# Folding the two key blocks of sliding-window attention into one row, and moving two weight low-parts to GpSimd

## The chip, the cores and the metric

One core of one Trainium2 chip runs the whole program. The metric is the device time in microseconds. The core's engines run side by side, each with its own instruction stream in a fixed order: TensorE (PE in the profile), VectorE (DVE), ScalarE (ACT), GpSimd (POOL), and SyncE (SP), which issues the weight loads. They hand work to each other through semaphores.

## The reference, cut to what matters

The program is a two-layer decoder trunk on 256 tokens of width 1024: a retention layer and a sliding-window attention layer, each between two SwiGLU blocks. The change touches only the window attention, which in the reference is:

```
qi = jnp.arange(WINDOW)[:, None]              # WINDOW = 128
kj = jnp.arange(2 * WINDOW)[None, :]
rel = qi + WINDOW - kj
...
sc = jnp.einsum('bqkgd,bjkd->bkgqj', qx, kx) * scale
valid = (rel >= 0) & (rel < WINDOW) & (blk * WINDOW + kj - WINDOW >= 0)
sc = jnp.where(valid[None, None, None], sc, NEG_INF)
p = jax.nn.softmax(jnp.concatenate([sc, sink_logits], axis=-1), axis=-1)[..., :-1]
return jnp.einsum('bkgqj,bjkd->bqkgd', p.astype(vx.dtype), vx)
...
return o @ w_o
```

There are 16 query heads and 2 key heads. Token block 0 sees only its own 128 keys. Query q of block 1 sees keys q+1 to 127 of block 0 and keys 0 to q of block 1: always 128 keys, and each position within a block exactly once.

## The kernel before, in words

Activations lie transposed, features on the 128 partitions and 256 tokens along the row. Every fp32 weight is split in two fp32r parts: ScalarE rounds a unit of 128x2048 from `stage` to `w_hi` (`split`, L339), VectorE subtracts to get `w_lo` (`split`, L658), and TensorE makes the three products that matter. Both tiles have four slots; SyncE loads the next unit of a slot when `lo_ready` says that its low part is made. All order is written out by hand, one list of calls for each engine; there is no scheduler.

The attention stage is the function `attention()` of each engine. It works in six softmaxes: `TWO_0A`, `TWO_0B`, `TWO_1A`, `TWO_1B` (token block 1, two blocks of keys, four heads each; the first digit is the key head) and `OWN_0`, `OWN_1` (token block 0, one block of keys, eight heads). For each:

- TensorE writes the mask into the score banks with a matmul of the identity (`masks`) and adds the scores (`head_scores`).
- VectorE reduces the maximum (`softmax_front`, L1036) and makes the exponent's bias with three tiny operations (L1038 to L1040). ScalarE makes the exponentials and their sums (`exps`, L532). VectorE (or, for `TWO_0A` and `TWO_0B`, ScalarE, L543) divides by the sum (`softmax_back`, L1055).
- TensorE transposes the probabilities (`transposed_p`, L1585), ScalarE moves them to `pt_own` or `pt_two` (`rows_of_p`, L556), TensorE multiplies by the values (`values`), and ScalarE and VectorE split the result in two parts of `o_t` (L563; `out_lo`, L1062).
- `q_scale` on VectorE (a reduce, L907, and some ten tiny operations, L910 and L663 to L672) makes the scale of each query head; `q_rope` (L847 to L853) rotates the queries.
- `wo_tiles` on TensorE is the output projection, four weight units `wo` 0 to 3, each waiting for its `w_lo` and its `o_t` part.

GpSimd only adds up squares for the norms (L1166 to L1189); it does nothing between 760.1 and 823.2 us. In all texts "two-input" means a VectorE operation whose two tensor operands both lie in SBUF, such as L658, L853, L1038 or L1055, in contrast to a reduce or to an operation that reads PSUM.

## Time and profile before

| | |
|---|---|
| median of 3 runs | 1015.26 us (1015.19 to 1015.81) |
| the profiled execution | 1015.4 us, its span 1013.6 us |
| TensorE busy | 1009.5 us, 100% of the span; granted clock 1.00 throughout |
| VectorE, ScalarE, GpSimd busy | 786.3, 497.2, 101.4 us |
| attention stage on TensorE | 756.9 to 826.7 us |

The profiled execution's own time is longer than its span by what lies before the first and after the last instruction, 1.8 us. Times of single instructions below are in microseconds from the span's start.

### The profile page before, as it was taken

The numbers are of one execution on the slowest core, as the hardware profiler recorded it, in microseconds if no ns is written. First come the engines' busy times: TensorE is split into PE (matmuls) and PEld (weight loads), VectorE is DVE, ScalarE is ACT, GpSimd is POOL, SyncE is SP. The second block draws the span as 40 slices with busy tenths as digits, with TensorE's granted clock in tenths as the row PEclk, the third lists the DMA queues.
The fourth block names the chain that finished last, engine by engine and source line by source line (L and its number), as shares of the span: only waits on it lengthen the run. The fifth ranks groups of instructions, "written<-read, shape, count | busy, mean of one in ns | idle before, by whom it ended". The sixth has DMA issues, their size and how long they took to land.

```text
span 1013.6 us, 15818 instructions
## 1 busy us (share of the span) xinstructions
PE 1009.5 (100%) x5916; PEld 886.5 (87%) x5916; DVE 786.3 (78%) x886; ACT 497.2 (49%) x537; POOL 101.4 (10%) x103
## 2 busy tenths in 40 slices
PE   9999999999999999999999999999999999999998
PEld 8888888888888888888888888888897898888888
DVE  7988866797797878777767787787778977977743
ACT  7455435544443354454444454464447944544432
POOL 0000013201101052000013100001220041000000
PEclk9999999999999999999999999999999999999999
DMA  9664456652542454555455645535562344644461
GB/s 348 242 237 177 143 174 218 246 197 104 218 195 97 193 171 173 212 190 180 150 179 199 246 166 201 191 135 172 187 244 115 110 160 188 208 168 166 156 193 64
DMA packets 32295, 185.31 MB, mean 183 GB/s; under 512 B 3840, under 2 KB 6400, under 8 KB 16128
## 3 DMA queue, kind: packets, MB, share of 16 engines
q1 hardware_dynamic: 31968, 184.64, 50.9%
q8 instruction: 23, 0.38, 0.2%
q10 hardware_dynamic: 288, 0.16, 0.1%
q14 instruction: 16, 0.13, 0.0%
HBM read 183.73 MB, written 1.05 MB: 182 GB/s over the span
## 4 chain that ended last, share of the span: by engine, by line
PE 100%; DVE 0%; issue 0%; DVEq 0%
PE ps L1219 99%; PE ps L1585 1%; PE ps L1552 0%; PE ps L1544 0%; DVE x L841 0%; DVE ones L1125 0%; DVEq L1126 0%
## 5 line engine op out<-in xcount | busy, mean ns | idle before, releaser
L1219 PE MATMUL ps<-h,w_hi 128*128 128x512 f32 x1664 | 556.1, 393 | 0.0
L1219 PE MATMUL ps<-h,w_lo 128*128 128x256 f32 x1664 | 430.8, 279 | 0.0
L658 DVE TENSOR_TENSOR w_lo<-stage,w_hi 128x2048 fp32r<-128x2048 f32 (+1 forms) x190 | 398.2, 2105 | 29.3 <-ACT w_hi L339 29.1
L1219 PEld LDWEIGHTS ps<-h,w_hi 128*128 128x128 f32 x1664 | 310.1, 188 | 66.9 <-DVE w_lo L658 0.2
L339 ACT ACTIVATE w_hi<-stage 128x2048 fp32r<-128x2048 f32 (+1 forms) x190 | 326.7, 1727 | 5.6 <-PE ps L1219 4.7
L1219 PEld LDWEIGHTS ps<-h,w_lo 128*128 128x128 f32 x1664 | 302.1, 189 | 3.5
L1219 PE MATMUL ps<-act_t,w_hi 128*128 128x512 f32 (+1 forms) x726 | 240.0, 386 | 0.0
L1219 PE MATMUL ps<-act_t,w_lo 128*128 128x256 f32 x704 | 190.1, 279 | 0.0
L1219 PEld LDWEIGHTS ps<-act_t,w_hi 128*128 128x128 f32 x726 | 134.4, 188 | 28.4
L371 ACT ACTIVATE tmp<-ps 128x1024 f32<-128x1024 f32 x44 | 45.1, 1026 | 189.2 <-PE ps L1219 189.2
L1219 PEld LDWEIGHTS ps<-act_t,w_lo 128*128 128x128 f32 x704 | 130.4, 189 | 0.3
L740 DVE TENSOR_TENSOR tmp<-ps,tmp 128x1024 f32<-128x1024 f32 x44 | 53.8, 1223 | 68.4 <-ACT tmp L371 68.4
L404 ACT ACTIVATE tmp<-ps 128x256 f32<-128x256 f32 x39 | 14.8, 380 | 118.9 <-PE ps L1219 118.9
L1219 PE MATMUL ps<-w_hi,h 128*128 128x512 f32 x192 | 60.3, 395 | 0.0
L786 DVE SCALAR_TENSOR_TENSOR tmp<-ps,tmp 128x256 f32<-128x256 f32 x39 | 16.4, 421 | 53.9 <-ACT tmp L404 53.9
L376 ACT ACTIVATE tmp<-tmp 128x512 f32<-128x512 f32 x44 | 27.9, 633 | 61.9 <-DVE tmp L746 61.9
L746 DVE TENSOR_TENSOR tmp<-tmp,r_row 128x1024 f32<-128x1024 f32 x44 | 53.9, 1225 | 1.5
L1166 POOL TENSOR_TENSOR sq_sum<-x 128x256 f32<-128x256 f32 x5 | 3.1, 614 | 479.2 <-DVE x L788 416.2
L1175 POOL TENSOR_TENSOR sq_sum<-sq_sum,sq 128x256 f32<-128x256 f32 x31 | 45.3, 1461 | 2.4
L1219 PE MATMUL ps<-y_t,w_hi 128*128 128x512 f32 x128 | 43.3, 392 | 0.0
L1219 PEld LDWEIGHTS ps<-w_hi,h 128*128 128x128 f32 x192 | 35.1, 188 | 7.8 <-issue 0.7
L715 DVE SCALAR_TENSOR_TENSOR h<-x,gain,h 128x256 fp32r<-128x256 f32 (+1 forms) x48 | 32.5, 677 | 10.2 <-ACT h L350 10.2
(172 smaller groups left out, 746.9 us busy)
## 6 DMA issues: line engine op xcount, KB each, us to landing
stage<-w_in_dram SPq DMA_DIRECT2D x85, 1024.0 KB, 4.8
stage<-w_out_dram SPq DMA_DIRECT2D x64, 704.0 KB, 4.0
stage<-w_ret_dram SPq DMA_DIRECT2D x24, 1024.0 KB, 4.9
stage<-w_ret_out_dram SPq DMA_DIRECT2D x8, 1024.0 KB, 4.8
stage<-w_q_dram SPq DMA_DIRECT2D x4, 1024.0 KB, 6.3
stage<-w_o_dram SPq DMA_DIRECT2D x4, 1024.0 KB, 4.9
stage<-w_in_dram SPq DMA_DIRECT2D x8, 256.0 KB, 4.2
stage<-w_in_dram SPq DMA_DIRECT2D x2, 512.0 KB, 6.1
```

Of the source, the lines that this page charges most:

```text
L339: nc.scalar.activation(w_hi[:, s, 0:n], stage[:, s, 0:n], ACT.Copy).then_inc(hi_ready, 1)
L371: nc.scalar.activation(t, ps[:, 4 * (g % 2):4 * (g % 2) + 4, T:2 * T], ACT.Copy).then_inc(in_lo_half, 1)
L376: nc.scalar.activation(tmp[:, g % 2, 0:512], tmp[:, g % 2, 0:512], ACT.Silu).then_inc(in_silu, 1)
L404: nc.scalar.activation(tmp[:, d % 2, 0:T], ps[:, bank, T:2 * T], ACT.Copy, scale=scale).then_inc(out_lo_half, 1)
L658: nc.vector.tensor_tensor(w_lo[:, s, 0:n], stage[:, s, 0:n], w_hi[:, s, 0:n].bitcast(F32), ALU.subtract).then_inc(lo_ready, 1)
L715: nc.vector.scalar_tensor_tensor(h[:, ds(d + per * i, 1), T:2 * T], x[:, ds(d + per * i, 1), :], gain[:, ds(m * DT + d + per * i, 1)], h[: ...
L740: nc.vector.tensor_tensor(t, ps[:, 4 * (g % 2):4 * (g % 2) + 4, 0:T], t, ALU.add).then_inc(in_free, 1)
L746: nc.vector.tensor_tensor(t, t, same(r_row[:], 4), ALU.mult).then_inc(in_scaled, 1)
L786: chain.step(nc.vector.scalar_tensor_tensor(t, ps[:, bank, 0:T], scale, t, ALU.mult, ALU.add))
L1175: nc.gpsimd.tensor_tensor(sq_sum[:], sq_sum[:], sq[:], ALU.add).then_inc(sum_added, 1)
L1219: return nc.tensor.matmul(out_, w, x_, start=start, stop=stop)
L1585: last = nc.tensor.transpose(ps[:, P_T_BANKS[e][r], q * P:(q + 1) * P], s[:, h0 + head, kb * P:(kb + 1) * P], ident[:])
```

## The change

Three things change in the attention stage.

1. The rows with two key blocks are folded to 128 keys. The scores of both blocks are made without a mask. In PSUM, VectorE copies the first block's scores over those of the second wherever the second's key lies after the query (`copy_predicated`), and the maximum, exponentials, scaling and transposes work on 128 keys instead of 256. After the transpose, the folded probabilities lie in the second half of `pt_two`; GpSimd multiplies them by a 0/1 mask into the first half and subtracts that from the second (`blocks_of_p`). `values` waits for `p_second` instead of `pt_ready`.
2. The low parts of `wo` units 0 and 1 are made by GpSimd in four quarters each (`low_part`) instead of by VectorE; VectorE keeps a wait at a later place (`low_part_made`), which passes the news on to `lo_ready`.
3. ScalarE makes the high part of `wo` unit 1 before the last transposed queries instead of after the first probabilities.

```
-    s_two = [at(f"s_two{c}", [P, CH, 2 * P], F32, ...) for c in range(2)]
+    s_two = [at(f"s_two{c}", [P, CH, P], F32, ...) for c in range(2)]
...
@@ VectorE, softmax_front
-                chain.step(nc.vector.tensor_reduce(mx.rearrange("q (i p) -> q i p", p=2), scores_by_head(e), AX.X,
-                                                   ALU.max))
+                by_head = scores_by_head(e)
+                if b:
+                    chain.step(nc.vector.copy_predicated(
+                        by_head[:, :, :, P:2 * P],
+                        mask[:, P:2 * P].bitcast(I32).rearrange("q (i p k) -> q i p k", i=1, p=1).broadcast_to(
+                            [P, n // 2, 2, P]), by_head[:, :, :, 0:P]))
+                    by_head = by_head[:, :, :, P:2 * P]
+                chain.step(nc.vector.tensor_reduce(mx.rearrange("q (i p) -> q i p", p=2), by_head, AX.X, ALU.max))
@@ VectorE, attention
                 q_rope(1, 0)
-                split(u)
                 q_rope(1, 1)
                 softmax_back(OWN_0)
+                low_part_made(0)
                 q_scale(1, 0, 2)
                 softmax_front(OWN_1)
                 out_lo(0)
                 softmax_front(TWO_1A)
-                split(u + 1)
                 softmax_back(OWN_1)
+                low_part_made(1)
                 softmax_front(TWO_1B)
@@ GpSimd
+            def low_part(j):
+                u = FIRST["wo", 0] + j
+                pool.wait_ge(hi_ready, u + 1)
+                for q in range(4):
+                    cols = slice(q * UNIT // 4, (q + 1) * UNIT // 4)
+                    nc.gpsimd.tensor_tensor(w_lo[:, u % SLOTS, cols], stage[:, u % SLOTS, cols],
+                                            w_hi[:, u % SLOTS, cols].bitcast(F32), ALU.subtract).then_inc(wo_lo, 1)
+            def blocks_of_p(n, e):
+                c, b, h0, heads = SOFTMAXES[e]
+                first, second = (pt_two[:, h0:h0 + heads, kb, :] for kb in range(2))
+                pool.wait_ge(pt_ready[e][0], 1)
+                nc.gpsimd.tensor_tensor(first, second, same(mask[:, 0:P], heads), ALU.mult).then_inc(p_first, 1)
+                pool.wait_ge(p_first, n + 1)
+                nc.gpsimd.tensor_tensor(second, second, first, ALU.subtract).then_inc(p_second, 1)
@@ TensorE, attention (the four masks() of TWO_0A, TWO_0B, TWO_1A, TWO_1B go; so do the second transposes)
-                masks(TWO_0A)
...
                 transposed_p(TWO_1A, 0)
-                transposed_p(TWO_1A, 1)
@@ TensorE, values
-                    pe.wait_ge(pt_ready[e][0], 1)
-                    pe.wait_ge(pt_ready[e][1], 1)
+                    pe.wait_ge(p_second, 2 * c + k % 2 + 1)
```

How the streams change at the places that matter. First VectorE around the queries of the second key head; `w_lo` is the low part of `wo` unit 0, `s_own` the probabilities of `OWN_0`. Before:

```order
L847 TENSOR_TENSOR q_a<-ps,tables 128x512 [waits q_squared10,q_done1,qt_done00]
L850 TENSOR_TENSOR q_b<-ps,tables 128x8x32 x2
L853 TENSOR_TENSOR q_a<-q_a,q_b 128x512 [waits dve_chain]
L658 TENSOR_TENSOR w_lo<-stage,w_hi 128x2048 [waits hi_ready]
L847 TENSOR_TENSOR q_a<-ps,tables 128x512 [waits used,qt_done01]
```

The same place of the changed kernel:

```order
L846 TENSOR_TENSOR q_a<-ps,tables 128x512 [waits q_squared10,q_done1,qt_done00]
L849 TENSOR_TENSOR q_b<-ps,tables 128x8x32 x2
L852 TENSOR_TENSOR q_a<-q_a,q_b 128x512 [waits dve_chain]
L846 TENSOR_TENSOR q_a<-ps,tables 128x512 [waits used,qt_done01]
```

The subtraction of 2048 columns is gone from VectorE here. GpSimd, which had nothing between two norm sums, now has sixteen operations of 512 columns in this stage (changed kernel):

```order
L1209 TENSOR_TENSOR w_lo<-stage,w_hi 128x512 [waits hi_ready]
L1209 TENSOR_TENSOR w_lo<-stage,w_hi 128x512 x3
L1217 TENSOR_TENSOR pt_two<-pt_two,mask 128x4x128 [waits pt_ready00]
L1219 TENSOR_TENSOR pt_two<-pt_two 128x4x128 [waits p_first]
L1217 TENSOR_TENSOR pt_two<-pt_two,mask 128x4x128 [waits pt_ready10]
L1219 TENSOR_TENSOR pt_two<-pt_two 128x4x128 [waits p_first]
L1209 TENSOR_TENSOR w_lo<-stage,w_hi 128x512 [waits hi_ready]
L1209 TENSOR_TENSOR w_lo<-stage,w_hi 128x512 x3
L1217 TENSOR_TENSOR pt_two<-pt_two,mask 128x4x128 [waits pt_ready40]
L1219 TENSOR_TENSOR pt_two<-pt_two 128x4x128 [waits p_first]
L1217 TENSOR_TENSOR pt_two<-pt_two,mask 128x4x128 [waits pt_ready50]
L1219 TENSOR_TENSOR pt_two<-pt_two 128x4x128 [waits p_first]
```

On TensorE, the values of `TWO_1A` (the own block's 4 matmuls, then the two blocks' 8) before:

```order
L1219 MATMUL ps<-pt_own,v_sb 64x128 [waits pt_ready30]
L1219 MATMUL ps<-pt_own,v_sb 64x128 x3
L1219 MATMUL ps<-pt_two,v_sb 64x128 [waits pt_ready41,pt_ready40]
L1219 MATMUL ps<-pt_two,v_sb 64x128 x7
```

and in the changed kernel:

```order
L1254 MATMUL ps<-pt_own,v_sb 64x128 [waits pt_ready30]
L1254 MATMUL ps<-pt_own,v_sb 64x128 x3
L1254 MATMUL ps<-pt_two,v_sb 64x128 [waits p_second]
L1254 MATMUL ps<-pt_two,v_sb 64x128 x7
```

The place in TensorE's order is the same; the wait has moved from ScalarE's copy to GpSimd's second operation behind it.

## Rows read from the trace of the kernel before

**Rows 1.** Windows, columns: stretch, length, busy PE, PEld, DVE, ACT, POOL, clock, DMA, GB/s.

```profile
765.00:805.00 40.00, 39.89 (x291) 32.63 (x291) 36.80 (x91) 33.93 (x94) 0.00 (x0) 1.00 0.28 103
```

**Rows 2.** Timeline of TensorE: start, length, instruction, count.

```profile
764.21 0.62 PE L1219 MATMUL ps<-mask_r,ident_r 128*128 128x512 f32 x2
764.66 0.50 PE L1219 MATMUL ps<-ones,sq_sum 128*128 128x2 f32 x4
...
776.83 0.60 PE L1552 MATMUL ps<-ident,q_a 128*128 128x128 f32 x4
...
786.31 1.91 PE L1585 MATMUL ps<-ident,s_two 128*128 128x128 f32 x16
787.98 0.71 PE L1219 MATMUL ps<-mask_r,ident_r 128*128 128x512 f32 x2
...
794.20 0.74 PE L1219 MATMUL ps<-mask_r,ident_r 128*128 128x512 f32 x2
794.86 1.13 PE L1219 MATMUL ps<-k_t,q_t 64*128 64x256 f32 x8
796.11 0.47 PE L1219 MATMUL ps<-o_t,w_hi 128*128 128x256 f32 x2
...
806.62 1.04 PE L1585 MATMUL ps<-ident,s_two 128*128 128x128 f32 x8
...
810.21 1.04 PE L1219 MATMUL ps<-pt_two,v_sb 128*64 128x128 f32 x16
```

**Rows 3.** Timeline of VectorE in the attention stage; in brackets, idle before and releaser.

```profile
765.93 0.69 DVE L907 TENSOR_REDUCE hs<-q_sq 128x8 f32<-128x512 f32 x1 [0.57 <-ACT q_sq L517]
...
768.82 1.22 DVE L1036 TENSOR_REDUCE sm<-ps 128x4 f32<-128x1024 f32 x1
...
774.58 0.68 DVE L847 TENSOR_TENSOR q_a<-ps,tables 128x512 f32<-128x512 f32 x1
...
775.96 0.69 DVE L853 TENSOR_TENSOR q_a<-q_a,q_b 128x512 f32<-128x512 f32 x1
...
793.32 0.17 DVE L672 SCALAR_TENSOR_TENSOR hs<-hs,hs 128x16 f32<-128x16 f32 x1
...
795.28 0.68 DVE L1062 TENSOR_TENSOR o_t<-ps,o_t 128x512 fp32r<-128x512 f32 x1
```

**Rows 4.** Timeline of ScalarE: exponentials, weight unit, probabilities of `TWO_1B`.

```profile
770.65 0.56 ACT L532 ACTIVATE s_two<-ps,sm,hs 128x256 f32<-128x256 f32 x1 [2.30 <-DVE sm L1040]
...
775.19 1.93 ACT L339 ACTIVATE w_hi<-stage 128x2048 fp32r<-128x2048 f32 x1
...
782.35 0.46 ACT L532 ACTIVATE s_own<-ps,sm,hs 128x128 f32<-128x128 f32 x1 [0.59 <-DVE sm L1040]
...
813.41 1.09 ACT L556 ACTIVATE pt_two<-ps 128x512 f32<-128x512 f32 x2 [1.42 <-PE ps L1585]
```

**Rows 5.** Timeline of GpSimd, in other stages.

```profile
145.88 0.61 POOL L1172 TENSOR_TENSOR sq<-x 128x256 f32 x1 [7.03 <-DVE x L788]
146.58 2.00 POOL L1175 TENSOR_TENSOR sq_sum<-sq_sum,sq 128x256 f32<-128x256 f32 x1
...
228.62 1.95 POOL L1204 TENSOR_TENSOR y_sq<-y_sq 128x512 f32<-128x512 f32 x1 [34.37 <-ACT y_sq L499]
230.65 0.74 POOL L1208 TENSOR_TENSOR sq_all<-y_sq 128x256 f32<-128x256 f32 x1
```

**Rows 6.** VectorE in those stretches, and near 29 us, beside GpSimd's L1196.

```profile
29.29 0.57 DVE L670 TENSOR_TENSOR n_t<-n_t,n_v 128x256 f32<-128x256 f32 x1
...
31.71 0.43 DVE L670 TENSOR_TENSOR n_t<-n_t,n_v 128x256 f32<-128x256 f32 x1
...
145.96 2.02 DVE L658 TENSOR_TENSOR w_lo<-stage,w_hi 128x1408 fp32r<-128x1408 f32 x1 [0.28 <-ACT w_hi L339]
...
148.78 1.61 DVE L658 TENSOR_TENSOR w_lo<-stage,w_hi 128x1408 fp32r<-128x1408 f32 x1
...
227.14 2.29 DVE L658 TENSOR_TENSOR w_lo<-stage,w_hi 128x2048 fp32r<-128x2048 f32 x1 [0.38 <-ACT w_hi L339]
```

More of the change, by code:

```diff
@@ L147, in trunk @@
     s_own = [at(f"s_own{c}", [P, CH, P], F32, (big + 16384, big)[c]) for c in range(2)]
-    s_two = [at(f"s_two{c}", [P, CH, 2 * P], F32, (big + 20480, base + 110592)[c]) for c in range(2)]
+    s_two = [at(f"s_two{c}", [P, CH, P], F32, (big + 20480, base + 110592)[c]) for c in range(2)]
     pt_own = at("pt_own", [P, CH, 1, P], F32, big + 28672)
@@ L234, in trunk @@
     p_scaled, p_ready = sem("p_scaled"), sem("p_ready")
+    p_first, p_second, wo_lo = sem("p_first"), sem("p_second"), sem("wo_lo")
     pt_done, pt_ready = ([[sem(f"{n}{e}{r}") for r in range(2)] for e in range(len(SOFTMAXES))]
@@ L255, in scores, with row_scores @@
         return ps[:, SCORE_BANKS[e][j % 2], i * keys(e):(i + 1) * keys(e)]
+    def row_scores(e, j):
+        return scores(e, j)[:, keys(e) - P:keys(e)]
     def scores_by_head(e):
@@ L548, in rows_of_p @@
                 c, b, h0, n = SOFTMAXES[e]
-                pt = pt_two if b else pt_own
-                heads = 4 // (1 + b)
-                first = h0 + heads * r
+                first = h0 + 4 * r
                 if c:
@@ L555, in rows_of_p @@
                 act.wait_ge(pt_done[e][r], 1)
-                nc.scalar.activation(pt[:, first:first + heads, :, :],
-                                     ps[:, P_T_BANKS[e][r], :].rearrange("p (a k n) -> p a k n", a=heads, n=P),
+                nc.scalar.activation((pt_two if b else pt_own)[:, first:first + 4, b, :],
+                                     ps[:, P_T_BANKS[e][r], :].rearrange("p (a n) -> p a n", n=P),
                                      ACT.Copy).then_inc(pt_ready[e][r], 1)
@@ L582, in attention @@
                 rows_of_p(TWO_0A, 0)
-                rows_of_p(TWO_0A, 1)
                 rows_of_p(TWO_0B, 0)
-                rows_of_p(TWO_0B, 1)
                 squares(1, 1)
+                split(u + 1)
                 heads_to_rows(1, 1)
@@ L599, in attention @@
                 rows_of_p(TWO_1A, 0)
-                rows_of_p(TWO_1A, 1)
                 rows_of_p(OWN_1, 1)
@@ L604, in attention @@
                 rows_of_p(TWO_1B, 0)
-                rows_of_p(TWO_1B, 1)
                 split(v + 1)
@@ L1055, in softmax_back @@
                 nc.vector.tensor_tensor(
-                    s, s, sm[:, e, 4, h0:h0 + n].rearrange("p (g a) -> p g a", a=1).broadcast_to([P, n, keys(e)]),
+                    s, s, sm[:, e, 4, h0:h0 + n].rearrange("p (g a) -> p g a", a=1).broadcast_to([P, n, P]),
                     ALU.mult).then_inc(p_ready, 1)
@@ L1064, in out_lo, with low_part_made @@
                                         dst[:, :, 0:T].bitcast(F32), ALU.subtract).then_inc(o_lo[k], 1)
+            def low_part_made(j):
+                dve.wait_ge(wo_lo, 4 * (j + 1))
+                dve.sem_inc(lo_ready, 1)
             def add_wo_tile(d):
@@ L1212, in _ @@
             square_sum(ATT)
+            low_part(0)
+            blocks_of_p(0, TWO_0A)
+            blocks_of_p(1, TWO_0B)
+            low_part(1)
+            blocks_of_p(2, TWO_1A)
+            blocks_of_p(3, TWO_1B)
             square_sum(5)
@@ L1558, in masks @@
                 c, b, h0, n = SOFTMAXES[e]
-                own = mask_r[:] if b else mask_r[:, P:2 * P]
                 for bank in SCORE_BANKS[e]:
-                    matmul(ps[:, bank, 0:n // 2 * keys(e)].rearrange("p (a n) -> p a n", a=n // 2), ident_r[:],
-                           same(own, n // 2), True, False)
+                    matmul(ps[:, bank, :].rearrange("p (a n) -> p a n", a=n // 2), ident_r[:],
+                           same(mask_r[:, P:2 * P], n // 2), True, False)
             def head_scores(e):
@@ L1570, in head_scores @@
                     last = matmul(scores(e, j), q_t[c][rows, j // 2, b * P:(b + 1) * P], k_t[rows, c, 0:keys(e)],
-                                  False, j >= h0 + n - 2)
+                                  bool(b), bool(b) or j >= h0 + n - 2)
                 last.then_inc(s_done, 1)
@@ L1661, in attention @@
                 head_scores(OWN_1)
-                pe.wait_ge(pt_ready[TWO_0B][0], 1)
-                pe.wait_ge(pt_ready[TWO_0B][1], 1)
-                masks(TWO_1A)
                 pe.wait_ge(q_squared[1][1], 1)
@@ L1668, in attention @@
                 transposed_p(OWN_0, 0)
-                pe.wait_ge(pt_ready[TWO_0A][1], 1)
                 transposed_p(OWN_0, 1)
+                pe.wait_ge(pt_ready[TWO_0B][0], 1)
                 head_scores(TWO_1A)
@@ L1677, in attention @@
                 pe.wait_ge(pt_ready[OWN_0][1], 1)
-                masks(TWO_1B)
                 head_scores(TWO_1B)
@@ L1699, in attention @@
                 wo_tiles(1, range(6, DT))
-                pe.wait_ge(pt_ready[TWO_1A][1], 1)
                 transposed_p(TWO_1B, 0)
-                transposed_p(TWO_1B, 1)
                 wo_tiles(2, range(4))
@@ L1735, in constants @@
     mask = np.where((rel >= 0) & (rel < P), 0.0, NEG).astype(f)
+    mask[:, 0:P] = np.arange(P)[:, None] > np.arange(P)[None, :]
     return rot, decay, np.ascontiguousarray(rope), mask, np.eye(P, dtype=f)
```

11 lines of the change are left out of this document (3 added, 8 removed).

## The prediction, made before the changed kernel was timed

> **What bounds the kernel now.** I read the windows first: from 765 to 805 us TensorE is busy 39.89 of 40 us, and VectorE 36.80, ScalarE 33.93, GpSimd 0 [rows 1]. TensorE sets the end, so work taken from it shows one for one, as long as nobody hands it work later. Then the timelines, to see how far the others are ahead. They aren't. The rotation of the first queries ends at 776.65 (775.96 + 0.69), and TensorE transposes them at 776.83 [rows 2, 3]. VectorE ends the first low part of `o_t` at 795.96, and TensorE starts the output projection at 796.11 [rows 2, 3]. VectorE is the second bound, 0.15 to 0.2 us behind, so each microsecond by which it gets later is a microsecond of TensorE.
>
> **What TensorE loses in work.** Four pairs of mask matmuls go. The first is worth 0.45 (764.21 to 764.66), the last 0.66 (794.20 to 794.86) [rows 2]; with 0.45 and 0.56 for those between, which I estimate from these two, 2.1 us. Of 32 transposes of two-block probabilities 16 go: 16 take 1.67 us (786.31 to 787.98) [rows 2], so 0.1 each, 1.6 us. Together 3.7 us: 2.9 before the output projection (2.1 and 8 transposes), 0.4 in each of `TWO_1A` and `TWO_1B`.
>
> **What ScalarE loses.** An exponential of 256 columns takes 0.56, of 128 takes 0.46 [rows 4]: 16 times 0.1. Its copies of probabilities halve from 8 to 4. Its own stream gets shorter; it waits for VectorE before and after.
>
> **What VectorE gets by the fold.** A front of two blocks reduced 1024 columns in 1.22 [rows 3]. Now it is a predicated copy of 512 columns, then a reduce of 512, 0.69 by the reduce of rows 3. No row shows a predicated copy. The nearest is 512 columns with one operand in PSUM, 0.68 [rows 3]; the other ends are 0 and 1.22, two passes over PSUM. I take 0.68: with the hand-over each front is 0.2 us longer. The first two lie before the rotation that TensorE waits for with 0.2 us to spare. TensorE, 0.9 us earlier by two mask pairs, waits for it at about 776.9: the gain of these two pairs is gone at once. The cost at 0 would be 0.7 less each, at 1.22 0.5 more each.
>
> **What GpSimd does to VectorE.** This decides. The 1408-column subtraction takes 1.61 alone (148.78), but 2.02 when a GpSimd operation began 0.08 us ahead of it (145.88 and 145.96): it waited until GpSimd had finished at 146.49. The next GpSimd operation took 2.00 and ended 0.60 after VectorE's end at 147.98 [rows 5, 6]. So each keeps the other out for a whole operation. Even short VectorE operations are kept out: 0.57 instead of 0.43 beside the small ones of GpSimd near 29 us [rows 6]. For 512 columns: GpSimd's ended 1.14 after VectorE's (230.57 against 229.43), and an unhindered one of 256 takes 0.74 against 0.60 behind a release [rows 5, 6]; so 1.28 alone, one every 1.36, of which it keeps VectorE out for 1.05.
> The Trainium skill (SBUF — State Buffer, section Who interferes with whom) says the same: a VectorE instruction with two inputs in SBUF contends with a GpSimd instruction that reads SBUF, and whoever issues first has the shared ports for the whole of it; one with at most one input there doesn't contend. The trace agrees where it has both engines at work, with the 2.02 and 2.00 above. It speaks against this change, which puts sixteen such GpSimd operations beside a VectorE that is 92% busy.
>
> The tiny operations of `q_scale` and the fronts are two-input, a chain with one every 0.2 us (0.17 and the hand-over). Between two GpSimd operations there is room for about one of them besides the one that waited; each GpSimd operation that meets the chain costs VectorE up to 1.05, on the mean 0.95.
>
> **Sum A, up to the output projection.** `wo` unit 0: its high part is ready at 777.1 less 0.8 of shorter exponentials (775.19 + 1.93) [rows 4], 776.4; four GpSimd operations last to 782.0. They meet the first sum of `softmax_sums` and the first and third two-input operation of `q_scale`: 3 x 0.95 = 2.85 us, of which 0.4 goes into idle time of VectorE before the reduce. With the 0.2 of the fronts, `softmax_front(OWN_0)` is 2.6 late. The subtraction of 2048 columns is gone, 2.2 back (2.29, less the overlap with the next) [rows 6], so at the probabilities of `OWN_0` VectorE is only 0.3 late. Then GpSimd gets the transposed probabilities at about 789.6 and runs eight operations without a pause to about 801: four of the fold, four of unit 1. Beside them VectorE has eight two-input operations of `q_scale(1, 0, 2)`, which before ended at 793.49 [rows 3], and three of the front of `OWN_1`: five waits, 4.3 us (the first is a part). `out_lo(0)` ends 4.6 late, at 800.5, and TensorE starts the projection at 800.55 instead of 796.11: **+4.45**, all of the 2.9 saved until there swallowed. The other removed subtraction stands behind this point and helps only later. Low parts 0 and 1 themselves are ready by 782 and 801, before their use at 800 and 809, so the later wait on VectorE costs nothing, and the loads that wait for `lo_ready` still come well ahead of their use at about 813 us and later.
>
> **Sum B, values of `TWO_1A`.** From the start of the transposes to the values, TensorE had 3.59 us of other work (806.62 to 810.21) [rows 2], now 3.2. In that time ScalarE copies (0.25 until the transposes are out, 0.6; two took 1.09 [rows 4]), and GpSimd multiplies and subtracts, 1.28 + 1.36. That alone is 0.5 to 0.9 too long. And VectorE is in its 2.28 us subtraction of unit 3, which it begins 0.5 before the multiply, and the multiply waits 1.6 for it. TensorE waits 2.5, less the 0.4 of transposes: **+2.1**.
>
> **Sum C, values of `TWO_1B`.** TensorE has 3.6 us of cover; the multiply meets the end of the first subtraction of the next layer (0.8), the subtract the whole of the second (1.9): 6.3 us of path. **+2.7 - 0.4 = +2.3**.
>
> A + B + C = 4.45 + 2.1 + 2.3 = 8.9 (rounded). Nothing after takes it back: TensorE is the bound from there on. 1015.4 + 8.9 = 1024.3 for a profiled execution; the median before is 0.14 below its own profiled execution, so 1024.2.
>
> **The rivals.**
> *Only large operations are kept out (1020).* No row has an operation of 8 or 16 columns beside a working GpSimd. If they slip through, VectorE loses in A only around the two rotations, 0.7 to 1 us, and gets 2.2 back; TensorE starts the projection about 0.2 late instead of 4.45. B and C stand: +0.2 + 2.1 + 2.3 = +4.6, 1019.9. For it: the chain reads hardly anything. Against: the 0.57 near 29 us is a 256-column operation held for GpSimd's time, not for its own.
> *The engines hardly hinder each other here (1015).* The fold's operations and quarters slip between; VectorE, 4.4 us of subtraction lighter, keeps its time. Then only the 0.2 of each front, GpSimd's own 2.64 against the cover in B (0.9) and short waits of 0.4 to 0.5 for the transposes of `OWN_0` and the projection count, 3.5 us against 3.7: -0.2, 1015.1. It would need GpSimd's operations to fall only where VectorE reads PSUM.
> *TensorE keeps what it saves (1012).* The same, and the predicated copy is nearly free, so that the waits at 776.9 and in B vanish: -3.7 at most, -2.5 as a middle, 1012.8. It decides from the point where VectorE isn't later at the projection than before. Rows 5 and 6 speak against it, and the 0.15 us of slack.
> *A dear predicated copy* (1.22) lies in the main case's range: +0.5 for each front, about +1.6 where they are on the path, 1025.8.
>
> **How the numbers follow.** The main case 60%, with its own range 1020.5 to 1027 (0.6 to 1.1 instead of 0.95 a wait, the copy between 0 and 1.22, one collision of B or C missed: -1.9). Only large ones 20%; hardly any 12%; TensorE keeps it 8%. The time is the main case's 1024.2. The range 1016.5 to 1027 leaves out most of the last two. A change of 0.2%, 2 us, is about what can be told from none. Faster: 0.09, same 0.11 (nearly all of the third case), slower 0.80.
>
> **What would show each step.** In the profile after: `mask_r` matmuls 4 instead of 12 and `s_two` transposes 16 instead of 32; copies of 0.6 to 0.8 on PSUM; VectorE's two-input operations of 8 or 16 columns between 777 and 801 with a few of 0.9 to 1.2 instead of 0.17 (A; none of them: the first rival); a gap of some 4 us on TensorE ahead of the first `o_t` matmul, and gaps of about 2.5 ahead of the `pt_two` values of `TWO_1A` and `TWO_1B` (B, C); GpSimd's operations at 1.3 alone and 2 to 3 beside a weight subtraction. If GpSimd's 512 columns take clearly less than 1.1, or TensorE has no gap there, the forecast is wrong.

## The result, and the profile after

The changed kernel takes 1028.58 us (median of 4 runs, 1027.86 to 1029.2), the kernel before 1015.23 beside it: ratio 1.0129, 95% interval 1.0116 to 1.0141. That is 13.3 us slower, where 9 were forecast. The profiled execution has a span of 1027.4 us against 1013.6, 13.8 more; its own time is 1029.2.

The windows of the changed kernel come first: stretch, length, busy TensorE, weight loads, VectorE, ScalarE, GpSimd, granted clock, DMA share, GB/s.

```profile
765.00:805.00 40.00, 30.03 (x194) 22.63 (x193) 37.22 (x77) 23.71 (x68) 15.77 (x12) 0.94 0.20 75
797.00:803.90 6.90, 0.00 (x0) 0.03 (x1) 6.55 (x13) 0.71 (x3) 3.64 (x3) 0.71 0.00 1
803.90:806.00 2.10, 2.09 (x10) 2.10 (x11) 1.64 (x5) 2.10 (x11) 0.00 (x0) 0.50 0.00 0
831.00:833.00 2.00, 2.00 (x12) 2.00 (x11) 0.69 (x1) 0.02 (x1) 0.00 (x0) 0.50 0.66 279
```

TensorE was busy 39.89 of the first 40 us [rows 1]; now it is idle for 9.97. VectorE is busy a little longer than before (37.22 against 36.80), though 4.5 us of weight subtractions left it. And in two stretches the granted clock is 0.50, 1.2 instead of 2.4 GHz, which the kernel before never shows there (its clock is 1.00 throughout).

The timeline of TensorE shows where that time lies, with idle time and releaser in brackets:

```profile
776.86 0.63 PE L1587 MATMUL ps<-ident,q_a 128*128 128x128 f32 x4 [0.42 <-DVE q_a L852]
...
803.91 0.77 PE L1254 MATMUL ps<-o_t,w_hi 128*128 128x256 f32 x2 [7.02 <-DVE o_t L1067]
...
806.74 1.09 PE L1254 MATMUL ps<-pt_two,v_sb 128*64 128x128 f32 x16
...
820.12 1.09 PE L1254 MATMUL ps<-pt_two,v_sb 128*64 128x128 f32 x16 [1.13 <-POOL pt_two L1219]
...
829.28 1.09 PE L1254 MATMUL ps<-pt_two,v_sb 128*64 128x128 f32 x16 [2.55 <-POOL pt_two L1219]
...
840.54 1.09 PE L1254 MATMUL ps<-h,w_hi 128*128 128x512 f32 x4
```

The same points in the kernel before are 776.83, 796.11 and 810.21 [rows 2], and these three:

```profile
797.70 1.09 PE L1219 MATMUL ps<-pt_two,v_sb 128*64 128x128 f32 x16
...
817.04 1.04 PE L1219 MATMUL ps<-pt_two,v_sb 128*64 128x128 f32 x16
...
826.74 1.09 PE L1219 MATMUL ps<-h,w_hi 128*128 128x512 f32 x4
```

How late TensorE is at each point, and what each stretch adds:

| point | before | after | late | added |
|---|---|---|---|---|
| output projection starts (A) | 796.11 | 803.91 | 7.80 | 7.80 |
| values of `TWO_0B`, after the projection's first 12 matmuls | 797.70 | 806.74 | 9.04 | 1.24, clock |
| values of `TWO_1A` (B) | 810.21 | 820.12 | 9.91 | 0.87 |
| values of `TWO_1B` (C) | 817.04 | 829.28 | 12.24 | 2.33 |
| first matmuls of the next layer | 826.74 | 840.54 | 13.80 | 1.56, mostly clock |

That is the whole difference. The first 12 matmuls of the projection take 2.83 us instead of 1.59, in the window where the clock is 0.50.

VectorE between the first rotation and the projection shows what became of its chain:

```profile
776.64 1.24 DVE L1052 TENSOR_TENSOR sm<-sm 128x4 f32<-128x4 f32 x1
...
778.01 1.12 DVE L1052 TENSOR_TENSOR sm<-sm 128x4 f32<-128x4 f32 x1
...
779.26 0.66 DVE L906 TENSOR_REDUCE hs<-q_sq 128x8 f32<-128x512 f32 x1
779.95 0.42 DVE L909 TENSOR_SCALAR hs<-hs,col_v 128x8 f32<-128x8 f32 x1
780.40 1.22 DVE L662 TENSOR_SCALAR hs<-hs 128x8 int32<-128x8 int32 x1
781.66 0.17 DVE L668 TENSOR_TENSOR hs<-hs 128x8 f32<-128x8 f32 x1
...
789.45 1.22 DVE L1060 TENSOR_TENSOR s_own<-s_own,sm 128x1024 f32<-128x1024 f32 x1
790.91 1.22 DVE L906 TENSOR_REDUCE hs<-q_sq 128x16 f32<-128x1024 f32 x1 [0.23 <-ACT q_sq L522]
792.16 2.26 DVE L909 TENSOR_SCALAR hs<-hs,col_v 128x8 f32<-128x8 f32 x2
794.45 0.17 DVE L662 TENSOR_SCALAR hs<-hs 128x16 int32<-128x16 int32 x1
794.66 1.13 DVE L668 TENSOR_TENSOR hs<-hs 128x16 f32<-128x16 f32 x1
795.82 1.19 DVE L669 TENSOR_TENSOR hs<-hs,hs 128x16 f32<-128x16 f32 x1
797.04 1.19 DVE L670 SCALAR_TENSOR_TENSOR hs<-hs 128x16 f32<-128x16 f32 x1
798.26 1.19 DVE L671 SCALAR_TENSOR_TENSOR hs<-hs,hs 128x16 f32<-128x16 f32 x1
799.49 1.18 DVE L666 SCALAR_TENSOR_TENSOR hs<-hs 128x16 f32<-128x16 f32 x1
```

and GpSimd in the same time and at the two later waits:

```profile
776.41 5.18 POOL L1209 TENSOR_TENSOR w_lo<-stage,w_hi 128x512 fp32r<-128x512 f32 x4 [16.49 <-ACT w_hi L344]
789.90 1.91 POOL L1217 TENSOR_TENSOR pt_two<-pt_two,mask 128x512 f32<-128x512 f32 x1 [8.31 <-ACT pt_two L559]
...
795.72 4.92 POOL L1209 TENSOR_TENSOR w_lo<-stage,w_hi 128x512 fp32r<-128x512 f32 x4
817.02 1.70 POOL L1217 TENSOR_TENSOR pt_two<-pt_two,mask 128x512 f32<-128x512 f32 x1 [16.38 <-ACT pt_two L559]
...
824.05 1.89 POOL L1217 TENSOR_TENSOR pt_two<-pt_two,mask 128x512 f32<-128x512 f32 x1 [3.99 <-ACT pt_two L559]
826.02 3.20 POOL L1219 TENSOR_TENSOR pt_two<-pt_two 128x512 f32<-128x512 f32 x1
```

Read the two side by side. An operation of 16 columns that took 0.17 in [rows 3] takes 1.19 as long as GpSimd works without a pause, and one VectorE operation gets through for each of GpSimd's (one every 1.22 us against 1.23 for a quarter). When GpSimd stops at 781.6, the chain runs at 0.17 again. The reduces (0.66 and 1.22) aren't held. Neither are the two reciprocals of 0.18 between the first rows, which the view has and the lines above leave out.

### The profile page after: what moved, and what is told of

The parts are those of the page before. It is cut to its first block, busy times and chain, and to the rows that moved or that the text cites. A ratio compares the mean times of both kernels' runs of the same rounds, so it can differ in the third digit from the quotient of the medians.

```text
span 1027.4 us, 15782 instructions
## 1 busy us (share of the span) xinstructions
PE 1009.5 (98%) x5892; PEld 884.8 (86%) x5892; DVE 791.5 (77%) x888; ACT 493.1 (48%) x533; POOL 127.5 (12%) x119
## 4 chain that ended last, share of the span: by engine, by line
PE 90%; DVE 5%; ACT 1%; POOL 1%; SPq 1%; DMA 1%; issue 0%; ACTq 0%; DVEq 0%
PE ps L1254 90%; DVE w_lo L657 1%; DMA stage<-w_in_dram 1%; POOL pt_two L1219 0%; DVE sm L1042 0%; ACT w_hi L344 0%; ACT s_own L537 0%; POOL pt_two L1217 0%; SPq L298 0%; DVE hs L909 0%; SPq L296 0%; DVE hs L906 0%; DVE hs L669 0%; DVE hs L670 0%; DVE hs L671 0%
## 5 line engine op out<-in xcount | busy, mean ns | idle before, releaser
L657 DVE TENSOR_TENSOR w_lo<-stage,w_hi 128x2048 fp32r<-128x2048 f32 (+1 forms) x188 | 394.1, 2106 | 28.9 <-ACT w_hi L344 28.6
L1182 POOL TENSOR_TENSOR sq<-x 128x256 f32 x31 | 28.6, 924 | 113.9 <-DVE x L787 112.3
```

Of the source, the lines that this page charges most:

```text
L657: nc.vector.tensor_tensor(w_lo[:, s, 0:n], stage[:, s, 0:n], w_hi[:, s, 0:n].bitcast(F32), ALU.subtract).then_inc(lo_ready, 1)
L1182: nc.gpsimd.tensor_tensor(sq[:].rearrange("p (a n) -> p a n", a=1), x[:, ds(i + 1, 1), :], x[:, ds(i + 1, 1), :], ALU.mult).then_inc(sq_do ...
```

## The experiments

All are set against the kernel before on the same chip. "Projection" is the first `o_t` matmul, "next layer" the first `h,w_hi` matmul of it (before: 796.11 and 826.74). The traces aren't aligned better than to half a microsecond: a VectorE row ahead of the stage, at 753.15 in the kernel before, stands between 752.95 and 753.49 in the others, so smaller differences between two traces mean little unless this start is taken off.

| run | median us | ratio to before, 95% | projection | next layer |
|---|---|---|---|---|
| the changed kernel | 1028.58 | 1.0129 (1.0116 to 1.0141) | 803.91 | 840.54 |
| low_on_vector | 1023.8 | 1.009 (1.0069 to 1.011) | 800.29 | 835.27 |
| low_on_gpsimd_alone | 1021.96 | 1.0064 (1.0047 to 1.008) | 801.01 | 833.20 |
| low_whole_units | 1031.62 | 1.0158 (1.0141 to 1.0175) | 805.52 | 842.73 |
| tensor_kept_busy | 1029.5 | 1.0131 (1.0114 to 1.0148) | 804.11 | 840.84 |
| tensor_kept_busy_2 | 1028.83 | 1.0128 (1.0111 to 1.0145) | 804.38 | 840.92 |
| idle_reads | 1024.24 | 1.0089 (1.0072 to 1.0106) | 803.17 | 835.35 |
| idle_writes | 1016.07 | 1.0005 (0.9995 to 1.0015) | 796.82 | 827.46 |
| one_gpsimd_step | 1019.75 | 1.0046 (1.003 to 1.0063) | 798.26 | 830.08 |
| fold_without_gpsimd | 1017.85 | 1.002 (1.0011 to 1.0029) | 797.96 | 829.28 |
| fold_second_head | 1015.17 | 0.9995 (0.9986 to 1.0004) | 795.94 | 826.30 |

**Each half of the change alone.** low_on_vector keeps the fold and gives the low parts back to VectorE:

```diff
                 softmax_front(OWN_0)
                 q_rope(1, 0)
+                split(u)
                 q_rope(1, 1)
                 softmax_back(OWN_0)
-                low_part_made(0)
...
                 softmax_front(TWO_1A)
+                split(u + 1)
                 softmax_back(OWN_1)
-                low_part_made(1)
...
-            low_part(0)
-            low_part(1)
```

> The fold alone: the low parts of wo units 0 and 1 are back on VectorE, at their old places. Theory (VectorE and GpSimd keep each other out for whole operations; while GpSimd has work, one VectorE operation gets through for each of its own, those of 8 columns and tensor_scalar among them): eight GpSimd operations less. Four of the fold still meet the probabilities of OWN_0 and the chain of q_scale, the projection starts 3 to 4 us later than before instead of 7.8, TWO_1A and TWO_1B cost 2 to 2.5 each: 1022.5 to 1025. Rival 1 (the 0.17 us operations get long for another reason than GpSimd, such as the changed place of ScalarE's high part, which stays changed here): the projection starts 7 to 8 us late as in the changed kernel, 1028. Rival 2 (only the eight operations of the low parts hurt, as they run without a pause): the projection starts on time, 1018 to 1020.

Measured: 1023.8, inside the range; the projection is 4.2 late, just over the 3 to 4 expected. Only four GpSimd operations lie ahead of it. VectorE of this kernel:

```profile
788.44 1.66 DVE L852 TENSOR_TENSOR q_a<-q_a,q_b 128x512 f32<-128x512 f32 x1
790.03 1.23 DVE L1052 TENSOR_TENSOR sm<-sm 128x8 f32<-128x8 f32 x1
...
791.53 2.02 DVE L1060 TENSOR_TENSOR s_own<-s_own,sm 128x1024 f32<-128x1024 f32 x1
```

Alone these take 0.69 [rows 3], 0.16 and 1.22: 2.8 us lost, right on the way to the transposes of `OWN_0`, for which TensorE waits 2.25. Of the rest, 0.3 lies ahead of the stage, 0.3 in the longer fronts, and 0.7 in `out_lo(0)`, which waits 0.63 for ScalarE's part of `o_t`, behind a TensorE whose clock is 0.53 from 794 to 797. The values of `TWO_1A` then wait 2.89, because the multiply began 0.1 into a weight subtraction (812.50 to 814.78) and met it in full:

```profile
812.61 3.29 POOL L1217 TENSOR_TENSOR pt_two<-pt_two,mask 128x512 f32<-128x512 f32 x1 [17.93 <-ACT pt_two L559]
```

low_on_gpsimd_alone is the other half, the kernel before with `low_part` and `low_part_made` of the change and nothing of the fold.

> The kernel before, with only the low parts of wo units 0 and 1 made by GpSimd in quarters; no fold. Theory: four quarters beside q_scale(0, 0, 1) cost VectorE 3 to 4 us less the 2.2 of the subtraction that is gone; four beside the front of OWN_1 and the last operations of q_scale(1, 0, 2) 3 to 4 us more; the projection starts 4 to 6 us late and TensorE's clock falls in the wait (1.2 us): 1020.5 to 1023. No gaps ahead of the values. Rival (GpSimd is a free helper when TensorE doesn't wait for its results): VectorE has 4.4 us less to do, 1013 to 1015.3.

Measured: 1021.96, projection 4.9 late behind a wait of 2.85 for `o_t`, both as expected. So each half alone is slower, by 0.9% and 0.64% (by the medians 8.3 and 6.4 us; one of low_on_vector's four times is 1027.45 and lifts its ratio). Together they cost 1.29%, a little less than their sum; why the rest of it goes missing wasn't taken apart. The earlier place of ScalarE's high part, the third thing that the change does, is in low_on_vector and not in low_on_gpsimd_alone, and both are slower. fold_without_gpsimd below keeps it too and loses 2.1 us in all, so it can't be what the change costs.

**How many operations, or how much time?** low_whole_units makes each low part in one GpSimd operation of 2048 columns:

```diff
-                for q in range(4):
-                    cols = slice(q * UNIT // 4, (q + 1) * UNIT // 4)
-                    nc.gpsimd.tensor_tensor(w_lo[:, u % SLOTS, cols], ...).then_inc(wo_lo, 1)
+                nc.gpsimd.tensor_tensor(w_lo[:, u % SLOTS, :], ...).then_inc(wo_lo, 4)
```

> The changed kernel, with each low part in one GpSimd operation of 2048 columns instead of four of 512. Theory: what VectorE loses is the time GpSimd has its operations, not their number: one VectorE operation is held for some 4.5 us instead of four for 1.2 each. Within 1 us of the changed kernel, 1027.5 to 1030. Rival (a fixed cost for each time they meet): six meetings less, 3 us or more faster, under 1026.

Measured: 1031.62, projection 805.52, 1.6 later than with quarters. GpSimd's time hardly differs (4.69 and 4.50 against 5.18 and 4.92), the number of meetings falls from eight to two, and it is slower:

```profile
776.81 4.69 POOL L1207 TENSOR_TENSOR w_lo<-stage,w_hi 128x2048 fp32r<-128x2048 f32 x1 [16.54 <-ACT w_hi L344]
...
797.13 4.50 POOL L1207 TENSOR_TENSOR w_lo<-stage,w_hi 128x2048 fp32r<-128x2048 f32 x1
```

```profile
776.97 4.54 DVE L1052 TENSOR_TENSOR sm<-sm 128x4 f32<-128x4 f32 x1
...
797.23 4.43 DVE L669 TENSOR_TENSOR hs<-hs,hs 128x16 f32<-128x16 f32 x1
```

Both numbers missed: the theory had whole units within 1 us of the quarters, the rival had them faster. The second fence is VectorE: one tiny operation waits for the whole unit, 4.4 us lost at the first and 4.3 at the second, where the quarters cost 3.3 and 4.1. At the first unit the quarters let a reduce and two reciprocals through, which aren't held, while a single unit has a held operation standing ahead of them for all its time. These 1.3 us, and 0.3 by which the trace is late before the stage, are the 1.6 at the projection. Behind it the clock also stays at 0.50 for longer, from 805.5 to past 810. What follows is that VectorE loses GpSimd's time, not an amount for each meeting.

**Reads without results.** idle_reads is the kernel before, with eight multiplies of 512 columns on GpSimd into a tile that nobody reads, from the moment the first two-block probabilities are copied:

```diff
             square_sum(ATT)
+            pool.wait_ge(pt_ready[TWO_0A][0], 1)
+            for i in range(8):
+                nc.gpsimd.tensor_tensor(spare..., same(mask[:, 0:P], 4), same(ident[:], 4), ALU.mult).then_inc(extra, 1)
+                pool.wait_ge(extra, i + 1)
             square_sum(5)
```

> The kernel before, plus eight GpSimd multiplies of 512 columns of SBUF into a spare tile, for which nobody waits, from the moment the first probabilities of TWO_0A are transposed. Theory (the two engines keep each other out over SBUF reads): though nothing depends on them, VectorE's scaling of s_own and its operations of 8 and 16 columns take 1.1 to 1.3 us each beside them, the projection starts 5 to 7 us later than 796.11, and a clock fall comes on top: 1021 to 1024. Rival (the changed kernel is slow because its engines wait for GpSimd's results): nobody waits here, 1015.3.

Measured: projection 7.06 late, 1024.24, a little above both forecasts, with no result for anyone to wait for. GpSimd, then VectorE, of this kernel:

```profile
787.72 11.97 POOL L1216 TENSOR_TENSOR spare<-mask,ident 128x512 f32<-128x512 f32 x8 [27.54 <-ACT pt_two L557]
```

```profile
795.77 1.19 DVE L664 TENSOR_SCALAR hs<-hs 128x16 int32<-128x16 int32 x1
797.00 0.18 DVE L670 TENSOR_TENSOR hs<-hs 128x16 f32<-128x16 f32 x1
797.21 1.13 DVE L671 TENSOR_TENSOR hs<-hs,hs 128x16 f32<-128x16 f32 x1
798.37 0.17 DVE L672 SCALAR_TENSOR_TENSOR hs<-hs 128x16 f32<-128x16 f32 x1
798.58 1.14 DVE L673 SCALAR_TENSOR_TENSOR hs<-hs,hs 128x16 f32<-128x16 f32 x1
```

Here every GpSimd operation waits for the one before it, one in 1.50 us on the mean, and two VectorE operations pass between two of them: 0.17 and 1.14 by turns. That is the pattern the forecast had assumed. In the changed kernel the four quarters follow each other with no wait between, and only one passes. That the wait makes this difference is argued: the operations differ in their operands too, and quarters with a wait between them weren't run. Nor does the pause lower the price. Before the rows shown, the last step of a rotation took 1.67 for 0.69, the first sum 1.24 for 0.16 and `s_own` 2.12 for 1.22, and the `TENSOR_SCALAR` pair behind the reduce 1.47 for 0.36. With the three held rows above that is seven waits for eight GpSimd operations, 7.0 us, which is all of the 7.06.

idle_writes is the same with `nc.gpsimd.memset(spare, 0.0)` in place of the multiply.

> The same with eight GpSimd memsets of 512 columns, which read nothing. Theory (it is reads that exclude): VectorE unchanged, 1015 to 1015.7. Rival (any GpSimd instruction, its dispatch or its semaphores holds VectorE up): VectorE's small operations long beside each memset, several microseconds slower.

Measured: 1016.07, 0.4 above the range, but no difference that can be told from none. VectorE beside the memsets (787.89 to 792.51):

```profile
789.10 1.23 DVE L1056 TENSOR_TENSOR s_own<-s_own,sm 128x1024 f32<-128x1024 f32 x1
790.25 1.21 DVE L908 TENSOR_REDUCE hs<-q_sq 128x16 f32<-128x1024 f32 x1
791.50 0.46 DVE L911 TENSOR_SCALAR hs<-hs,col_v 128x8 f32<-128x8 f32 x2
791.99 0.54 DVE L664 TENSOR_SCALAR hs<-hs 128x16 int32<-128x16 int32 x1
```

Three two-input operations lie beside the memsets and all keep their time: 0.69, 0.16 and 1.23, where idle_reads has 1.67, 1.24 and 2.12 for the same three. So it is GpSimd's reading that shuts the two-input operations out, not its being at work. The `TENSOR_SCALAR`s are held by the writes as well, 0.46 instead of 0.36 and 0.54 instead of 0.18, and these 0.46 us are what the projection is late by once the 0.24 ahead of the stage are taken off. The memsets are shorter than the multiplies, 4.6 us for eight against 12.0, and are over before the chain of 16 columns begins; it was not run beside writes.

**What the clock is worth.** tensor_kept_busy is the changed kernel with matmuls that nobody reads, 28 ahead of the projection and 11 ahead of the values of `TWO_1B`:

```diff
                 pe.wait_ge(pt_ready[OWN_0][1], 1)
+                filler(3, 28)
                 wo_tiles(0, range(2))
...
                 values(OWN_1, 3)
+                filler(2, 11)
                 values(TWO_1B, 3)
```

> The changed kernel, with matmuls of the mask that nobody uses (28 of 512 columns ahead of the output projection, 11 ahead of the values of TWO_1B) while TensorE waits there. Theory (after the two long gaps the granted clock was 0.50 for 2 to 4 us, which cost 1.2 and 1.5 us beside the waits themselves): the clock stays at 1.00, the start of the projection and the values stay where they are, and the end comes 2.3 to 2.8 us sooner: 1025.8 to 1026.5. Rival (the slower matmuls after the gaps have another reason, such as waiting for weights): no change, 1028.5, the o_t matmuls after the waits still 0.21 apart.

tensor_kept_busy_2 has the same 28, and 8 ahead of the values of `TWO_1A` instead of the 11.

> The changed kernel with the 28 matmuls ahead of the output projection, and 8 ahead of the values of TWO_1A instead of the 11 ahead of TWO_1B. In the first such run the first clock fall went (1.0 us back), the values of TWO_1A then waited longer and the clock fell there, and the 11 matmuls ran 2.7 us past the end of a wait that was over. Theory (the clock is a cost of its own, 1.2 to 1.5 us for each fall): clock 1.00 up to the values of TWO_1B, 1025 to 1027. Rival (what the clock gives back is lost again in the collisions of GpSimd with the weight subtractions, which shift): 1027.5 to 1029.

Measured: 1029.5 and 1028.83, nothing gained. The clock did what was expected at the projection: the first 12 matmuls took 1.60 (804.11 to 805.71) instead of 2.83. The 1.2 us were lost again 12 us later. TensorE of the first, then GpSimd of the first:

```profile
804.11 0.48 PE L1254 MATMUL ps<-o_t,w_hi 128*128 128x256 f32 x2 [0.52 <-DVE o_t L1067]
...
820.29 1.25 PE L1254 MATMUL ps<-pt_two,v_sb 128*64 128x128 f32 x16 [2.32 <-POOL pt_two L1219]
...
828.35 2.80 PE L1254 MATMUL ps<-mask_r,ident_r 128*128 128x512 f32 x11
```

```profile
816.00 2.90 POOL L1217 TENSOR_TENSOR pt_two<-pt_two,mask 128x512 f32<-128x512 f32 x1 [15.16 <-ACT pt_two L559]
```

TensorE came 1 us sooner to the transposes of `TWO_1A`, the multiply sooner too, and now it began 0.5 instead of 1.7 into the weight subtraction of unit 3 and took 2.90 instead of 1.70. The values start at 820.29, where the changed kernel started them at 820.12, and behind this wait of 2.32 the clock falls again (0.58 from 822 to 825). My forecast for the first (1025.8 to 1026.5) had counted the clock and not the collision that sits behind it.

The first run is no fair test of the second clock fall. Its 11 matmuls begin only at 828.35, GpSimd's last product is there at 828.38, and the values of `TWO_1B` start at 831.08: the filling itself cost the 2.7 us. The second run is clean there: its 8 matmuls are over before the product of `TWO_1A` is, the clock is 1.00 from 804 to 808 and from 820 to 824, and the values of `TWO_1A` still start no sooner (820.60, in a trace that is 0.4 late before the stage). It falls to 0.50 only behind the wait of 2.55 for `TWO_1B`. For this run I had named the rival that the collisions take back what the clock gives, and it held.

**The fold with less of GpSimd.** one_gpsimd_step is low_on_vector without the second GpSimd operation. The product with the other values is the difference of the two value blocks, made once:

```diff
-                nc.gpsimd.tensor_tensor(first, second, same(mask...), ALU.mult).then_inc(p_first, 1)
-                pool.wait_ge(p_first, n + 1)
-                nc.gpsimd.tensor_tensor(second, second, first, ALU.subtract).then_inc(p_second, 1)
+                nc.gpsimd.tensor_tensor(first, second, same(mask...), ALU.mult).then_inc(p_second, 1)
...
-                                          v_sb[:, c, kb, :], pt[...], kb == 0, kb == b)
+                                          v_diff[:, c, :] if b and kb == 0 else v_sb[:, c, kb, :], pt[...], kb == 0, kb == b)
```

> The kernel with the fold and the low parts on VectorE (low_on_vector), where GpSimd makes only the first product: TensorE multiplies the unsplit folded probabilities by the values of block 1 and the masked part by the difference of the values of both blocks (one 128x128 subtraction more). GpSimd's subtraction goes from each of the four. Theory (the path through GpSimd is 1.28 and 1.36 us in a row, plus one collision; B and C are that path less TensorE's cover of 3 us; two exclusions less ahead of the projection): the gap ahead of the values of TWO_1B goes, that of TWO_1A shrinks to 1.3 to 2 us, the projection starts 3 to 4 late: 1018 to 1020.5, against 1023.8. Rival (the collision with VectorE's subtraction alone makes the gaps, the length of the path doesn't matter): gaps as before, 1022.5 to 1024.

Measured: 1019.75, inside the range; the projection is 2.15 late, less than the 3 to 4 expected. The values of `TWO_1A` wait 1.56 for GpSimd, those of `TWO_1B` not at all, as expected. Half of the GpSimd operations, half of the loss (4.2 us against 8.3 by the medians).

fold_without_gpsimd gives VectorE the masked product too:

```diff
                 softmax_back(OWN_0)
+                masked_p(TWO_0A)
+                masked_p(TWO_0B)
                 q_scale(1, 0, 2)
...
-                nc.gpsimd.tensor_tensor(first, second, same(mask[:, 0:P], heads), ALU.mult).then_inc(p_second, 1)
...
+            def masked_p(e):
+
+                c, b, h0, n = SOFTMAXES[e]
+                if c:
+                    dve.wait_ge(o_done[h0 // 4], 2)
+                dve.wait_ge(pt_ready[e][0], 1)
+                nc.vector.tensor_tensor(pt_two[:, h0:h0 + n, 0, :], pt_two[:, h0:h0 + n, 1, :],
+                                        same(mask[:, 0:P], n), ALU.mult).then_inc(p_second, 1)
```

> The fold of all four two-block tiles stays, the low parts are VectorE's, and the masked product is VectorE's too (four multiplies of 512 columns, about 0.7 us each); GpSimd makes only one small subtraction before them (the difference of the two value blocks). So no GpSimd operation of 512 columns is left beside VectorE's scale, rope and subtraction work. Theory (what costs is GpSimd and VectorE reading at the same time): VectorE has about 0.7 + 0.7 of extra work ahead of the projection and 1.0 of predicated copies, against 2.15 us by which one_gpsimd_step started the projection late; projection 1.0 to 1.8 us late (797.1 to 797.9), the values of TWO_1A and TWO_1B wait under 0.7 each, total 1015.5 to 1017.5. Rival (the fold costs by its longer chain, copy, product, values, whoever makes the product): the values wait as in one_gpsimd_step (1.56) and the time stays 1019 to 1020.5.

Measured: 1017.85, 0.2% slower, 0.35 above the range I gave. The values wait nowhere. What is left is VectorE's own work ahead of the projection, and a clock fall behind the wait that it makes. VectorE, then TensorE, then a window of TensorE alone (busy, clock, DMA share, GB/s):

```profile
790.41 1.28 DVE L1071 TENSOR_TENSOR pt_two<-pt_two,mask 128x512 f32<-128x512 f32 x2
```

```profile
797.96 0.47 PE L1261 MATMUL ps<-o_t,w_hi 128*128 128x256 f32 x2 [2.32 <-DVE o_t L1077]
```

```profile
800.00:802.00 2.00, 2.00 (x21) 0.50 0.00 0
```

The chain is 1.85 late at `out_lo(0)` (797.13 against 795.28 [rows 3]): 1.2 of it are the two products, 0.4 the two fronts of `TWO_0` with the start of the trace (0.14), 0.27 an idle. With VectorE's four products at 0.64 to 0.69 instead of GpSimd's eight operations the loss falls from 8.3 to 2.1 us by the medians. The rival, that the longer chain of the fold costs as much whoever makes it, is out.

fold_second_head leaves the first key head as it was and folds only `TWO_1A` and `TWO_1B`, whose work lies mostly behind the projection's start. Masked product on VectorE, one small GpSimd subtraction for the value difference.

```diff
+    def folded(e):
+        return SOFTMAXES[e][0] and SOFTMAXES[e][1]
...
-                masks(TWO_1A)
...
-                masks(TWO_1B)
...
-                transposed_p(TWO_1A, 1)
...
-                transposed_p(TWO_1B, 1)
...
                 softmax_back(TWO_1B)
+                masked_p(TWO_1A)
                 split(u + 3)
                 out_lo(2)
+                masked_p(TWO_1B)
```

> The kernel before, with the fold for the second key head alone (TWO_1A, TWO_1B): no mask matmuls and half the probability transposes there (0.4 us of TensorE for each of the two, after the projection has begun), masked product by VectorE in two multiplies of 512 columns, the difference of the value blocks by one small GpSimd subtraction, nothing changed ahead of the projection but two predicated copies of 0.69 us on VectorE (one of them maybe ahead of it). Theory (TensorE's saving is kept where nothing it needs gets later): projection 0 to 0.5 us late, values do not wait, total 0.3 to 0.8 us under the kernel before (1014.4 to 1015.0). Rival (VectorE has no room for 2 x 0.69 + 2 x 0.7 there, and the values of TWO_1A or the low parts of units 3 and 4 come late): 1016 to 1018, with a wait of TensorE on the masked product or on the low part of a unit after 806.

Measured: 1015.17 against 1015.73 for the kernel before on that chip, 0.05% faster with an interval that includes none (0.9986 to 1.0004), and 0.2 above the range I gave. The trace has the next layer at 826.30, 0.44 earlier, of which 0.17 was there before the stage. TensorE:

```profile
795.94 0.48 PE L1246 MATMUL ps<-o_t,w_hi 128*128 128x256 f32 x2 [1.17 <-DVE o_t L1083]
```

The two mask pairs that it saves ahead of the projection turn into 1.17 of idle, since `o_t` comes no sooner. Only the transposes behind it are kept. It is the only version with a fold that isn't slower, and it can't be told from the kernel before.

## Why the prediction was wrong in size

**TensorE's saving (3.7, of it 2.9 ahead of the projection): about right.** From 765 to the projection TensorE worked 31.0 us before (796.11 - 765 - 0.11 idle) and 28.9 after (803.91 - 765 - 9.97), and the pair at 764.21 lies ahead of 765: 2.1 + 0.45 = 2.5. As forecast, all of it was swallowed.

**The predicated copy (0.68): right.** It takes 0.69, and the first rotation is waited for at 776.86 (forecast 776.9). In part that is luck: each front got longer by 0.1 to 0.2, but the trace was 0.2 early before the stage.

**Sum A (4.45, measured 7.80): the step that failed first.** The mechanism held: TensorE waits for `out_lo(0)` behind a VectorE chain that GpSimd keeps out, and one wait costs about what the forecast had (0.95). What was mis-sized is the number of waits, eight forecast and eleven measured, one of them short. It comes from two sentences: that there is room for about one operation "besides the one that waited", and that the tiny operations which count are the two-input ones. At the first unit the forecast had three waits, 2.85. Measured are 1.24, 1.12, 0.42 and 1.22 for 0.15, 0.13, 0.23 and 0.17, together 3.3: the last two are `TENSOR_SCALAR`s, which I had left out and which are held as well. At the second meeting the forecast had five waits, 4.3. Measured: the `TENSOR_SCALAR` pair 2.26 for 0.36, one 1.13 and four of 1.18 or 1.19 for 0.17 to 0.18, seven waits and 6.9 us. Followed along the chain, the first meeting made the miss hardly larger, as idle time of VectorE took up 0.5 of it: `s_own` is 0.6 late (forecast 0.3). Then come 0.3 of waiting for ScalarE's squares, which the forecast lacked, and 6.9 instead of 4.3.

How much of the 2.6 at the second meeting belongs to each of the two sentences isn't shown. The pair alone is 1.9. The rest goes with only one operation passing beside each quarter. But in idle_reads, where two pass, eight GpSimd operations cost seven waits and 7.0 us too.

The Trainium skill (SBUF — State Buffer, section Who interferes with whom) has more than the prediction took from it. Its sentence on instructions with at most one input in SBUF holds only outside the modes that use both port pairs, a condition that the prediction left out. A `tensor_scalar` can enter such a mode and so can contend as well, while a `tensor_reduce` on this chip never does. The runs agree on each point: 1.22 for 0.17 beside GpSimd's reads, 0.54 for 0.18 beside its memsets, and a reduce that stays at 1.21 beside both. Read to its end, the section would have put the `TENSOR_SCALAR`s of `q_scale`, two at the first meeting and three at the second, among the operations that can wait; four of the five did.

**Sum B (2.1, measured 0.87): right when it stands alone, too large beside the clock.** The forecast let the multiply begin 0.5 into the weight subtraction of unit 3 and wait 1.6. In the changed kernel it began 1.74 into it (817.02, VectorE's row starts at 815.28 and ends at 817.57) and took 1.70, 0.4 more than alone. The clock fall ahead of it had made TensorE later by 1.24, and that took most of the collision away. With the fall filled up, in tensor_kept_busy, the multiply began 0.5 into the subtraction and took 2.90, 1.6 more than alone, and the stretch from the projection to the values of `TWO_1A` cost 2.1, as forecast. Some luck is in the 2.1: the terms listed for the path add to 3.5 against 3.2 of other work, 0.3 too long and not 0.5 to 0.9. By the rows of the changed kernel, less the collision, they are about 4 against 3.3, since from the start of the transposes to the multiply it took 1.37 and not 0.85.

**Sum C (2.3, measured 2.33): right, with errors that cancel.** The multiply took 1.89 (0.6 lost, forecast 0.8), the subtraction 3.20 (1.9 lost, forecast 1.9). The path was 6.6 us where 6.3 was forecast, again by the copy, and TensorE had 4.05 of other work instead of 3.6.

**The clock (nothing forecast, measured 1.24 and about 1.5): the second step that failed.** The forecast had waits of 4, 2.5 and 2.5 us on TensorE and put what the clock does behind them at nothing, without a reason. Behind 7.02 it is 0.50 for 2.8 us, behind 2.55 for 3.4. Both falls together are 2.75 us. They can't simply be bought back: with the first one filled up, the collision in B took the gain.

So 8.9 forecast is 13.8 measured in the span: +3.35 in A, -1.2 in B, +2.75 by the clock. The terms aren't independent. The first clock fall and the shortfall of B are the same 1.2 us, as the two runs with the clock kept up show, so that what the change costs beyond the forecast is the 3.35 of A and the 1.5 of the second fall. By this sum A alone gives 1027.6, already just above the range; no run took the last 1.5 away without another cost.

**The rivals.** "Only large operations are kept out" is refuted by the 16-column operations at 1.19. "Hardly hinder each other" and "TensorE keeps what it saves" fell with the same rows. Three things stay open: whether a single GpSimd operation costs the same however its operands lie, whether waits between the quarters would change their price, and what a version costs that puts GpSimd's reads only beside VectorE's reduces, which it doesn't hold. None of them was tried.

## What to carry to other kernels

Work handed to GpSimd isn't off VectorE when both read SBUF. Here VectorE lost about GpSimd's whole time wherever it had operations with two inputs in SBUF, or `TENSOR_SCALAR`s, to do; reduces and reciprocals went on. It costs most where VectorE runs a chain of tiny operations that somebody waits for. Count GpSimd's duration for each of its operations that meets such a chain, and put the work on VectorE itself if it takes less there than on GpSimd: four products of 0.64 to 0.69 there cost 2.1 us in all, eight GpSimd operations 8.3. Letting GpSimd's operations fall beside reduces should cost little, by the rows, but no run tried it. A long wait that a change puts on TensorE is to be priced with the slow clock that can follow it, 1.2 to 1.5 us here for waits of 2.55 and 7.02.
